# A hybrid attention and SSD encoder block on one core: weight conversion five chunks ahead, and the two directions' diagonal blocks of an SSD head summed on TensorE

## The reference

```python
h = rms_norm(x, norm_mix_g)
u = h @ w_in                       # q | k | v | z | x B C | dt, 12352 columns
...
Lmat = jnp.exp(segsum(ac))         # inside a chunk of 128 tokens, per head
cb = jnp.einsum('bclgn,bcsgn->bgcls', Cc, Bc)
y_diag = jnp.einsum('bgcls,bghcls,bcsghp->bclghp', cb, Lmat, xc)
...
y_fwd = ssd_chunked(xs, dt[:, :, 0], A[0], Bm, Cm)
y_bwd = flip(ssd_chunked(flip(xs), flip(dt[:, :, 1]), A[1], flip(Bm), flip(Cm)))
y = y_fwd + y_bwd + xs * d_skip
...
x = x + concat(attn, ssd) @ w_out
x = x + square(relu(rms_norm(x, norm_mlp_g) @ w_up)) @ w_down
```

## Time and profile before

| what | value |
| --- | --- |
| median of 3 runs | 1597.03 us (1596.88 to 1598.89) |
| the profiled execution's own time | 1597.19 us |
| its span, first to last instruction | 1595.5 us |
| PE (TensorE matmul) busy | 1538.2 us, 96% of the span |
| DVE (VectorE) busy | 979.7 us, 61% |
| ACT (ScalarE) busy | 778.2 us, 49% |
| mean DMA rate over the span | 183 GB/s |
| mean granted TensorE clock | 0.991 of full speed |

### The profile page before, as it was taken

The page is one execution under the profiler, slowest core; times in us unless marked ns, Lnnn a source line. Parts: engine busy times, 40 slices in busy tenths (PEclk is TensorE's granted clock), DMA queues, the critical chain, the costliest instruction groups (busy, mean ns, idle before and its releaser), DMA issues.

```text
span 1595.5 us, 25920 instructions
## 1 busy us (share of the span) xinstructions
PE 1538.2 (96%) x9501; PEld 1377.2 (86%) x9501; DVE 979.7 (61%) x1362; ACT 778.2 (49%) x1075; POOL 24.2 (2%) x29
## 2 busy tenths in 40 slices
PE   6999899888999999999999999999999999999998
PEld 6999888886788888888889998899988998889987
DVE  5787788888876666665466555455554455535553
ACT  4377666666655545444344443334433444334432
POOL 0000000000101010000000000000000000000000
PEclk9999999999999999999999999999999999999999
DMA  9875556555565656565656656656565655656552
GB/s 256 257 222 163 144 157 181 164 168 172 150 195 166 185 174 183 177 236 169 197 185 179 181 181 198 185 172 185 186 197 170 182 183 192 192 167 184 185 195 95
DMA packets 186336, 291.59 MB, mean 183 GB/s; under 512 B 13533, under 2 KB 67151, under 8 KB 185984
## 3 DMA queue, kind: packets, MB, share of 16 engines
q1 hardware_dynamic: 183748, 285.92, 59.1%
q10 hardware_dynamic: 2492, 4.36, 0.9%
HBM read 288.04 MB, written 5.34 MB: 184 GB/s over the span
## 4 chain that ended last, share of the span: by engine, by line
PE 79%; DVE 11%; issue 5%; ACT 3%; DVEq 1%; DMA 0%; ACTq 0%
PE psum L1150 77%; DVE w_lo L770 2%; DVE mix L784 2%; DVE conv L804 2%; ACT w_hi L465 1%; ACT L532 1%; DMA x_in<-in_x 0%; DVE conv L800 0%; DVE cbm L815 0%; ACT conv_t L507 0%; PE psum L1249 0%; PE psum L1269 0%; PE psum L1195 0%; DVE gate_t L822 0%; DVE gate_t L845 0%
## 5 line engine op out<-in xcount | busy, mean ns | idle before, releaser
L770 DVE TENSOR_TENSOR w_lo<-raw,w_hi 128x1024 fp32r<-128x1024 f32 x512 | 625.1, 1224 | 501.7 <-ACT w_hi L465 496.2
L465 ACT ACTIVATE w_hi<-raw 128x1024 fp32r<-128x1024 f32 x512 | 539.7, 1057 | 654.5 <-PE psum L1150 651.4
L1150 PE MATMUL psum<-actT_lo,w_hi 128*128 128x256 f32 x1792 | 516.0, 288 | 16.8 <-DVE w_lo L770 16.8
L1150 PE MATMUL psum<-actT_hi,w_lo 128*128 128x256 f32 x1792 | 511.8, 286 | 0.0
L1150 PE MATMUL psum<-actT_hi,w_hi 128*128 128x256 f32 x1792 | 511.4, 285 | 0.0
L1150 PEld LDWEIGHTS psum<-actT_lo,w_hi 128*128 128x128 f32 x1792 | 348.7, 195 | 26.0 <-DVE w_lo L770 19.1
L1150 PEld LDWEIGHTS psum<-actT_hi,w_lo 128*128 128x128 f32 x1792 | 348.7, 195 | 0.2
L1150 PEld LDWEIGHTS psum<-actT_hi,w_hi 128*128 128x128 f32 x1792 | 348.8, 195 | 0.0
L1150 PE MATMUL psum<-w_hi,hid_lo 128*128 128x512 f32 x512 | 199.2, 389 | 0.0
L1150 PE MATMUL psum<-w_lo,hid_hi 128*128 128x512 f32 x512 | 199.2, 389 | 0.0
L1150 PE MATMUL psum<-w_hi,hid_hi 128*128 128x512 f32 x512 | 199.2, 389 | 0.0
(11 more groups left out here) (192 smaller groups left out, 1150.7 us busy)
## 6 DMA issues: line engine op xcount, KB each, us to landing
raw<-in_w_in SPq DMA_DIRECT2D x128, 512.0 KB
raw<-in_w_up SPq DMA_DIRECT2D x128, 512.0 KB
raw<-in_w_down SPq DMA_DIRECT2D x128, 512.0 KB
raw<-in_w_out SPq DMA_DIRECT2D x64, 512.0 KB
raw<-in_w_in SPq DMA_DIRECT2D x64, 256.0 KB
raw<-in_w_in SPq DMA_DIRECT2D x128, 128.0 KB
decay<-decay_rows SPq DMA_DIRECT2D x16, 512.0 KB, 5.7
rel_tiles<-rel_rows ACTq DMA_DIRECT2D x1, 3072.0 KB, 18.9
```

The source lines that it names most:

```text
L465: act.activation(w_hi[j % RING][:, :, :], raw[j][:, :, :], ACT.Copy).then_inc(hi_ready, 1)
L770: tt_(w_lo[i][:, :, :], raw[j][:, :, :], w_hi[i][:, :, :].bitcast(f32), ALU.subtract).then_inc(lo_dve, 1)
L1150: return pe.matmul(o, lhsT, rhs, start=first, stop=last, **kw)
```

## The change

Two edits. First, `w_lo[j]` is placed over `raw[j]` (the low part overwrites the loaded chunk), so `w_hi` and `w_lo` have 8 buffers each in the space that 8 + 4 + 4 took. The load of `raw[j]` now waits until TensorE has used the weight chunk (`chunk_used`), ScalarE's `high` waits for the load alone, and `LEAD` is 5. Second, `mix_head` leaves out the addition (and the semaphore `scaled`); TensorE multiplies the backward diagonal blocks by themselves, with two more matmuls of 128 columns per head that accumulate into the same output, and it takes one head after the other.

```diff
-RING = 4
-LEAD = 3
+LEAD = 5
...
+        raw_at = [top[0] + 4 * KC * UNIT * j for j in range(CH)]
         raw = [place(f"raw{j}", [P, KC, UNIT]) for j in range(CH)]
-        w_hi = [place(f"w_hi{j}", [P, KC, UNIT], f32r) for j in range(RING)]
-        w_lo = [place(f"w_lo{j}", [P, KC, UNIT], f32r) for j in range(RING)]
+        w_lo = [place(f"w_lo{j}", [P, KC, UNIT], f32r, at=raw_at[j]) for j in range(CH)]
+        w_hi = [place(f"w_hi{j}", [P, KC, UNIT], f32r) for j in range(CH)]
...
             def load(U, j, pieces):
                 if positive(U):
-                    wait_low(sp, U - 1, j)
+                    sp.wait_ge(chunk_used, CH * (U - 1) + j + 1)
...
             def high(U, j):
                 act.wait_ge(raw_in[j], 48 * (U + 1))
-                if positive(CH * U + j - RING + 1):
-                    act.wait_ge(chunk_used, CH * U + j - RING + 1)
-                act.activation(w_hi[j % RING][:, :, :], raw[j][:, :, :], ACT.Copy).then_inc(hi_ready, 1)
+                act.activation(w_hi[j][:, :, :], raw[j][:, :, :], ACT.Copy).then_inc(hi_ready, 1)
...
             def low(U, j):
-                i = j % RING
                 dve.wait_ge(hi_ready, CH * U + j + 1)
-                tt_(w_lo[i][:, :, :], raw[j][:, :, :], w_hi[i][:, :, :].bitcast(f32), ALU.subtract).then_inc(lo_dve, 1)
+                tt_(w_lo[j][:, :, :], raw[j][:, :, :], w_hi[j][:, :, :].bitcast(f32), ALU.subtract).then_inc(lo_dve, 1)
...
                     ins = stt_(w[:, k0:k1, :], w[:, k0:k1, :], tokp[:, src, ds(col, 1)], cbm[:, k0:k1, :],
                                ALU.mult, ALU.mult)
-                ins.then_inc(scaled, 1)
-                dve.wait_ge(scaled, H + 1)
-                tt_(w[:, 0:6:5, :], w[:, 0:3:2, :], w[:, 3:6:2, :], ALU.add).then_inc(mix_ready, 1)
+                ins.then_inc(mix_ready, 1)
...
                         pe.wait_ge(mix_ready, 4 * G + k - 2)
-                        for t in range(TT):
-                            for h in (k - 4, k - 3):
-                                ins = mm(M0[64 * (h % 2):64 * (h % 2) + 64, SEQ * (h // 2):SEQ * (h // 2 + 1)],
-                                         xtok[:, t, 64 * h:64 * h + 64], mix[h][:, 4 * t:4 * t + 2, :],
-                                         t == 0, t == TT - 1)
-                                if t == TT - 1:
-                                    ins.then_inc(y_done, 1)
+                        for h in (k - 4, k - 3):
+                            rows, c0 = slice(64 * (h % 2), 64 * (h % 2) + 64), SEQ * (h // 2)
+                            for t in range(TT):
+                                mm(M0[rows, c0:c0 + SEQ], xtok[:, t, 64 * h:64 * h + 64],
+                                   mix[h][:, 4 * t:4 * t + 2, :], t == 0, False)
+                            for t in range(TT):
+                                ins = mm(M0[rows, c0 + P * t:c0 + P * t + P], xtok[:, t, 64 * h:64 * h + 64],
+                                         mix[h][:, 3 - t, :], False, t == TT - 1)
+                            ins.then_inc(y_done, 1)
```

More of the change, by code:

```diff
@@ L248, in build @@
         decay_in = sem("decay_in")
-        args_ready, decays_ready, scaled, mix_ready, y_done = (sem(n) for n in (
-            "args_ready", "decays_ready", "scaled", "mix_ready", "y_done"))
+        args_ready, decays_ready, mix_ready, y_done = (sem(n) for n in (
+            "args_ready", "decays_ready", "mix_ready", "y_done"))
         x_transposed, xtok_ready, cb_done, cb_masked = (sem(n) for n in (
@@ L1164, in chunk_by_weights @@
                         for n, (w, a) in enumerate(((w_hi, actT_lo), (w_lo, actT_hi), (w_hi, actT_hi))):
-                            ins = mm(res[:, c, :], w[i][:, kk, cols], a[:, k, :],
+                            ins = mm(res[:, c, :], w[j][:, kk, cols], a[:, k, :],
                                      k == 0 and n == 0 and c % 2 == 0,
@@ L1179, in chunk_by_tokens @@
                         for n, (a, w) in enumerate(((lo, w_hi), (hi, w_lo), (hi, w_hi))):
-                            ins = mm(bank_pair(pair)[:, t, :], a[:, k0 + k, toks], w[i][:, kk, :],
+                            ins = mm(bank_pair(pair)[:, t, :], a[:, k0 + k, toks], w[j][:, kk, :],
                                      k == 0 and n == 0, k == KT - 1 and n == 2)
```

## The result

The changed kernel takes **1604.93 us**, the median of 10 runs (1601.05 to 1608.36); the kernel before took 1597.2 in 10 runs beside it (1596.01 to 1600.49). The ratio is **1.0041, with a 95% interval from 1.0029 to 1.0052**: slower by some 6 to 7 us, by more than the 0.2% that can be told from no change. The time lies at the upper edge of the predicted range, 0.07 us inside it, where the slower rival (1605) stood; the likeliest case, 1597.3, did not happen.

A forecast was written before the change was run, and what follows sets the result against it. VectorE's chain through ScalarE was taken to bound the SSD groups, at 44.0 us a period. Terms 3.4 - 9.3 + 3.2 + 2.5 + 0.5 = +0.3 gave 1597.3 us; range 1594 to 1600, for 8 in 10 1589.5 to 1605.

The forecast's parts named there:

- the slower rival: SSD groups: VectorE's gate at k=7 waits for PE's longer slots (`y_done`), half clock hitting all six periods; 1605 us, chance 0.30.
- T2 to T8: Six periods between k=4 slot starts of SSD groups two to eight: four at -1.75 us, two at -1.15, together -9.3.
- T1 to T2: From first to second SSD group's k=4 slot: late `decay` landing puts the gate near 129.0, 4.3 later, less 0.9: +3.4 us.
- the 2.85 us of the sum: PE's slot of two heads, one after the other: 2.85 us, 1.6 more than before; bounds 1.7 and 3.7.
- half clock: PE's slots behind some three waits over 2 us, half of them at 1.2 GHz: +2.5 us (0 to +10).
- The last group: Eighth SSD group: its two longer slots lie where PE is the bound again, +3.2 us.
- The output projection: SyncE passes the `xres` load three chunks later, into the loads behind attention's last head: +0.5 us (0 to 2).
- Start and attention: Start: later loads covered by five chunks, 0 (up to +2); attention: PE always busy, so nothing VectorE sheds pays there.
- MLP: Steps between the MLP's quarters: `down_add` stays ahead of the next conversion, so the 2.63 us stay three times: 0.
- The faster one: Rival for the SSD groups: `decay` landings and half clock cost nothing, -6.1 us, 1591 us; chance 0.30.
- It doesn't do what it says: Rival: conversions run no further ahead, PE's `w_lo` waits stay some 10 us; 1597 us, chance 0.40 together with the forecast.
- The three signs: Gate waiting for PE well over 11.5 us after the blocks; `w_hi` waiting for `raw`; new PE idling in attention, output or MLP.

The follow-up runs named there:

- mix_pairs: The kernel before with only the heads' edit (addition dropped, two more matmuls per head), the two heads alternating in every step; 1588.85 us, ratio 0.9946.
- after_hold: The changed kernel with the last three loads of the first unit in looped MLP quarters held until TensorE used the quarter's first chunk; 1602.54 us, ratio 1.0021.
- ring_only: The changed kernel with the addition back on VectorE and the slots as before, so the ring and lead edit alone; 1603.78 us, ratio 1.0031.
- mix_only: The kernel before with only the heads' edit, one head after the other, ring and lead as before; 1594.16 us, ratio 0.9975.
- after_pairs: The changed kernel with a slot's two heads alternating in the long and in the short matmuls; 1597.26 us, ratio 0.9992.

## Why the prediction was right or wrong

**The forecast as a whole.** The sum gave +0.3 us and the spans differ by 8.1. That the time still lies inside the stated range, by 0.07 us, is luck: it is not there by the sum, and only in part by the rival that stood at that edge. The step that failed is the gain of the six periods from T2 to T8.

**T1 to T2: right in mechanism, and in size by two misses that cancel.** Predicted +3.4 us, from a landing 6 us after the slot and a gate near 129.0, 4.3 us later than before, less 0.9 in the chain to the next blocks; measured +3.5, with ScalarE's arguments released by the load as said. But the gate came only 3.8 us later after its slot (13.1 against 9.3), and the chain behind it gave 0.3 us (31.5 against 31.7), not 0.9. The runs with slot 8 confirm it from the other side: with the load there in time T2 moved from 161.0 to 157.1. PE's slot was shorter than the 2.85 us of the sum (2.57). The estimate of 1.3 us a head from the columns holds: in the trace's single records the starts of the long matmuls lie 0.22 us apart and those of the short ones 0.11. What the sum had too much lies where the heads meet: the second head's first long matmul starts at 172.096 us, next to the first head's first short one (172.090), so that the heads overlap by some 0.4 us there and not by 0.11.

The Trainium skill's rule ("TensorE: Matmul & The Clock Gate", The mechanism), that matmuls start and end in program order, gave nearly the right size for this kernel, 2.57 and not 1.7. This case's trace does not keep to it strictly: the second head's long matmul at 172.096 us starts ahead of the first head's last short one (172.309), which stands before it in the program. And with the heads alternating the same records lie side by side throughout, 1.66 us.

**T2 to T8: the step that failed.** Predicted -9.3 + 2.5 = -6.8 us, measured -1.2. Two of its terms were mis-sized. From a gate to the next k=4 slot the sum took 0.9 us off each time, 5.4 in six; measured were 34.6, 31.3, 34.4, 31.3, 31.1 and 30.7 us, in the kernel before 34.3, 31.7, 34.3, 31.7, 31.9 and 31.6: 2.2 us less. The two numbers with a loop step in them did not fall at all, and that cost was in no step of the prediction: the loop step is 0.9 to 1.1 us longer there. From a k=4 slot to the gate the sum took 11.5 us, six times, with 1.2 for landings and 2.5 for half clock on top, 72.7 in all; measured were 13.7, 13.5, 12.0, 12.4, 11.6 and 11.2, together 74.5 (73.5 before): 1.0 more where some 1 less was forecast. The half clock was put at half of three waits over 2 us; it came behind three of PE's waits for blocks (3.06, 4.01 and 4.89 us, in T2, T3 and T5) with slots of 4.59, 4.59 and 3.94 us, and a fourth time in part in the last group (a wait of 2.21 us at T8, a slot of 3.54).

The shortening on VectorE itself was sized right: from a head's four scaling instructions to the next conversion it is 1.32 us (1.31 predicted), and in mix_pairs the whole chain from gate to blocks is 30.9 us (30.8 predicted) where no loop step lies in it. In the changed kernel the wait of the first head's scaling for the mask (`cbm`) is longer, and so is that of `cat_lo` for `cat_hi`:

```profile
249.24 1.41 DVE L782 SCALAR_TENSOR_TENSOR mix<-mix,tokp,cbm 128x256 f32<-128x256 f32 x4 [0.57 <-DVE cbm L811]
```

It is 0.22 us in mix_pairs, 1.59 us against 1.50 for `cat_lo`; together they are the 31.3 against 30.9.

**The reasons for that size.** By the rows, a wait of PE, a fall of the clock, a slot of 4.6 us and a wait of the gate follow from each other in the changed kernel, and what follows from each other need not add up. By the table of ratios (times 1597) the heads' edit is worth -4.0 us and the ring edit +5.0 by themselves; together they should cost 1.0, and they cost 6.5, a surplus of 5.5, which is more than the intervals of the four ratios allow (some 3). With alternating heads it is -8.6 and +5.0 against -1.3, a surplus of 2.3, which is within them. So the table shows that the two edits do not add up with one head after the other; that the slots' length decides how much the ring edit costs is likely by the medians but not shown, and the chain of wait, clock and slot is the reading of the rows above.

**The last group: right in the main,** +4.0 us for +3.2. **The output projection:** +0.1 for +0.5. **Start and attention:** 0, right. **PE busy:** +18.7 us for "some 20". **No `w_lo` waits:** right, and worth nothing, as said.

**MLP: wrong,** 0 predicted, +1.7 measured. The argument, that `down_add` stays ahead of the conversion, was right but not sufficient: two of the three loop steps are longer, 3.79 and 3.42 us of idle time of PE instead of 2.73. Without the loads in flight (after_hold) they are 2.73 and 2.88 and the 1.6 us come back; but the same loads cost nothing in ring_only, so it takes the heads' edit too.

**The rivals.** The slower one came out in time but only in part by its own mechanism. The gate does wait for PE, but three times and 5.3 us in all, not in all six periods. The rest of the time came from loop steps, in the windows (2 us) and in the MLP (1.7 us), and from a chain between gate and blocks that shrank by less than 0.9 us. The three signs that the prediction had named for being wrong all came: the gate waits for PE 13.7 and 13.5 us after the blocks, ScalarE's `w_hi` wait for `raw` (7.5 us, the longest 3.8 at 112.04 us, before the first group), and PE idles longer in the MLP. The waits for `raw` did not move T1 (115.5 in both kernels); five converted chunks did cover them there, as the prediction had said. The faster one fell with the landings. "It doesn't do what it says" fell with PE's `w_lo` waits.

**What stays open.** Late q14 packets explain the long loop steps of the runs with `decay` loads at slot 8 to 10, and the second packet goes with the changed kernel's 3.45 and 3.17 us at the windows' step, where its first packet is as early as in the kernel before (0.44 and 0.18 us, against 0.42 and 0.39): so that cost belongs to the heads' edit, and mix_only has it as well (3.72 and 3.60). Why the edit brings a second packet was not tried; the program of VectorE is shorter by the additions and its fetches fall at other places, but that is an argument and no run. Open, too, is why the changed kernel's first scaling waits 0.35 us longer for the mask, and why the same loads lengthen the MLP's steps with the heads' edit and not without it. The changed ring with slot 11's `decay` load well clear of the step was not run.

## What to carry to other kernels

Where two matmuls write different halves of the partitions, put them next to each other: the same work took 1.66 us instead of 2.57, and at half clock the difference doubles (4.52 us from the first record to the next matmul in the changed kernel, 2.76 in after_pairs). Before a buffer is reused in place, ask when its next load can start: a ring that is deeper on the conversion side was shallower on the load side, and the first group's `decay` load, behind it in the queue, was issued 10.5 us later. Keep large loads clear of the moment at which an engine goes back to the top of a loop: moving two 512 KB loads by one slot cost 4.2 us.

## What the runs showed of the hardware

An instruction fetch is a transfer in the DMA queues: VectorE's first instruction behind a loop step comes 1.9 to 2.8 us after the last of q14's packets starts, in all 28 steps. It comes late behind data: 5.0 to 7.0 us of idle time with two 512 KB loads in flight, 2.3 to 4.3 otherwise. The profile's releaser there is a `w_hi` long done, or "issue". Matmuls whose outputs lie on different partition halves overlap when they are neighbours in the program: 16 records lie in 1.52 us against 2.43, and where only the last and the first of two heads are neighbours, only those overlap. The clock was at 1.2 GHz, for the whole slot or a part of it, behind PE's waits of 2.48 and 2.94 us in the kernel before and of 3.06, 4.01 and 4.89 in the changed one; but the length of the wait alone does not tell. In the kernel before the slots behind waits of 2.47 us (337.61) and 3.03 us (381.74) ran at 2.4 GHz:

```profile
381.74 1.08 PE L1150 MATMUL psum<-mix,xtok 128*64 128x256 f32 x8 [3.03 <-DVE mix L788]
```

In mix_only one slot behind a wait of 2.00 us ran at 1.2 GHz (292.18) and one behind 2.01 us at 2.4 GHz (203.89). The slots of mix_pairs, whose longest such wait is 2.06 us, all took the 1.52 us of full clock.
